# A hybrid decoder block: the mixer's order table made anew

## The reference, cut to what matters

```python
# (A) GLA, per chunk: decay from a low-rank gate, causal scores, a state that is carried on
bc = jnp.cumsum(ac, axis=3)
o_inter = jnp.einsum('bhcd,bhde->bhce', qi * jnp.exp(bi), state)
scores = jnp.einsum('bhid,bhjd,bhijd->bhij', qi, ki, decay)      # decay = exp(bi - bj), causal
o_intra = jnp.einsum('bhij,bhje->bhie', scores, vi)
new_state = jnp.exp(b_last)[..., None] * state + jnp.einsum('bhcd,bhce->bhde', k_dec, vi)
o_gla = rmsnorm(o_gla, gla_norm_g[l]) * jax.nn.silu(g)
# (B) convolution: gate, 31 taps per channel, norm over channel groups, swish
u = c_in * jax.nn.sigmoid(c_gate)
u = causal_depthwise_conv(u, conv_w[l], conv_b[l])
o_conv = jax.nn.silu(channel_group_norm(u, conv_norm_g[l], conv_norm_b[l]))
h = h + jnp.einsum('bse,ed->bsd', jnp.concatenate([o_gla, o_conv], axis=-1), w_out[l])
ff = jnp.square(jax.nn.relu(jnp.einsum('bsd,df->bsf', rmsnorm(h, norm2_g[l]), w_mlp_in[l])))
h = h + jnp.einsum('bsf,fd->bsd', ff, w_mlp_out[l])
```

## Time and profile before

| | |
|---|---|
| median of 3 runs | 2025.66 us (2024.34 to 2025.87) |
| profiled execution, its own time | 2024.25 us |
| its span | 2022.2 us |
| PE busy in the span | 2000.1 us, 99% |
| DVE, ACT, POOL busy | 1473.9, 956.6, 445.9 us |

### The profile page before, as it was taken

The page is one execution under the profiler, slowest core; times in us unless marked ns, Lnnn a source line. Parts: engine busy times, 40 slices in busy tenths (PEclk is TensorE's granted clock), DMA queues, the critical chain, the costliest instruction groups (busy, mean ns, idle before and its releaser), DMA issues.

```text
span 2022.2 us, 27147 instructions
## 1 busy us (share of the span) xinstructions
PE 2000.1 (99%) x9898; PEld 1635.4 (81%) x9898; DVE 1473.9 (73%) x2178; ACT 956.6 (47%) x1361; POOL 445.9 (22%) x593
## 2 busy tenths in 40 slices
PE   8999999999999999999999999999999999999998
PEld 7787778787877778888888888888888888888887
DVE  3899978887878978877789777777664646545475
ACT  4456664355244563565557645554332333323253
POOL 5553475235126441000000000000020201202031
PEclk9999999999999999999999999999999999999999
DMA  6884458555555555444445433335967557565674
GB/s 227 285 289 152 139 202 295 167 168 186 198 200 191 179 208 191 162 146 144 148 163 206 153 122 127 126 121 197 376 231 266 188 203 265 181 220 185 206 239 177
DMA packets 175268, 395.76 MB, mean 196 GB/s; under 512 B 15424, under 2 KB 64672, under 8 KB 174624
## 3 DMA queue, kind: packets, MB, share of 16 engines
q1 hardware_dynamic: 154688, 317.47, 46.3%
q10 hardware_dynamic: 20448, 76.56, 10.8%
HBM read 301.70 MB, written 92.27 MB: 195 GB/s over the span
## 4 chain that ended last, share of the span: by engine, by line
PE 90%; DVE 6%; issue 2%; ACT 2%; POOL 0%; DMA 0%; DVEq 0%; ACTq 0%; POOLq 0%
PE acc L83 24%; PE acc L85 24%; PE acc L84 24%; PE acc L2565 3%; PE acc L2566 3%; PE acc L2567 3%; DVE acc L1724 2%; PE acc L2625 1%; PE acc L2520 1%; PE acc L2519 1%; PE acc L2521 1%; PE acc L2284 1%; ACT ring_hi L1355 1%; PE acc L2658 1%; DVE ring_sum L1869 1%
## 5 line engine op out<-in xcount | busy, mean ns | idle before, releaser
L1986 DVE TENSOR_TENSOR down_lo<-down_raw,down_hi 128x1536 fp32r<-128x1536 f32 x112 | 200.5, 1790 | 231.1 <-ACT down_hi L1441 231.1
L84 PE MATMUL acc<-down_lo,down_hi 128*128 128x512 f32 x896 | 348.5, 389 | 0.0
L83 PE MATMUL acc<-down_hi 128*128 128x512 f32 x896 | 348.5, 389 | 0.0
L85 PE MATMUL acc<-down_hi,down_lo 128*128 128x512 f32 x896 | 348.5, 389 | 0.0
L1441 ACT ACTIVATE down_hi<-down_raw 128x1536 fp32r<-128x1536 f32 x112 | 166.7, 1488 | 360.8 <-PE acc L85 192.9
L1724 DVE SCALAR_TENSOR_TENSOR acc<-u_sb,cw_col,acc 128x512 f32<-128x512 f32 x464 | 312.9, 747 | 0.3
L1355 ACT ACTIVATE ring_hi<-ring_sum 128x512 fp32r<-128x512 f32 x155 | 97.8, 631 | 250.3 <-DVE ring_sum L1869 247.9
L83 PE MATMUL acc<-xT_hi,wt 128*128 128x512 f32 x512 | 203.6, 398 | 0.7 <-ACT q_sb L1534 0.7
L1100 POOL TENSOR_TENSOR rows_a<-rows_a,second 128x512 f32<-128x512 f32 x20 | 25.3, 1296 | 803.6 <-ACT second L1449 655.5
L84 PE MATMUL acc<-xT_lo,wt 128*128 128x512 f32 x512 | 199.5, 390 | 0.0
L85 PE MATMUL acc<-xT_hi,wt 128*128 128x512 f32 x512 | 199.5, 390 | 0.0
(11 more groups left out here) (304 smaller groups left out, 4113.2 us busy)
## 6 DMA issues: line engine op xcount, KB each, us to landing
wt<-w_kept SPq DMA_DIRECT2D x168, 512.0 KB, 3.3
down_raw<-f_kept ACTq DMA_DIRECT2D x109, 512.0 KB, 4.3
raw_w<-in_w_mlp_in SPq DMA_DIRECT2D x32, 1024.0 KB, 5.9
f_kept<-f_tile SPq DMA_DIRECT2D x128, 256.0 KB, 2.0
down_raw<-in_w_mlp_out SPq DMA_DIRECT2D x64, 512.0 KB, 3.6
w_kept<-wt SPq DMA_DIRECT2D x48, 512.0 KB, 5.3
down_raw<-in_w_mlp_out SPq DMA_DIRECT2D x64, 256.0 KB, 3.2
down_more<-f_kept ACTq DMA_DIRECT2D x29, 512.0 KB, 5.3
```

What stands on the lines that cost most here:

```text
L83: nc.tensor.matmul(out, w_hi, x_hi, start=first, stop=False, skip_group_check=onto)
L84: nc.tensor.matmul(out, w_hi, x_lo, start=False, stop=False, skip_group_check=onto)
L85: return nc.tensor.matmul(out, w_lo, x_hi, start=False, stop=last, skip_group_check=onto)
L1986: nc.vector.tensor_tensor(down_lo[slot][:, :], down_raw[d % DOWN_RAW][:, 512:], down_hi[slot][:, :].bitcast(F32), ALU.subtract).then_inc(d ...
```

## The change

Only the list `ORDER` differs. It has 808 entries, where there were 761: the same steps, but the 496 taps, in the same sequence, are cut into 141 entries, where there were 94. The weight units keep their sequence. Against the other entries of the same engine, 59 of PE's 327 steps, 60 of DVE's 212 (taps apart), 95 of ACT's 261 and 31 of POOL's 122 have another place. The diff, cut to the places that the text speaks of:

```diff
-    (-1, "conv_gate_a", 2), (0, "taps", 0, 1, 6), (-1, "make_wz"), (0, "x_load", 2), (-1, "conv_gate", 2),
...
-    (0, "taps", 0, 32, 5), (0, "gate", 0), (0, "qk", 0), (-1, "make_masks", 2), (0, "x_load", 3),
...
-    (0, "gla_scores", 0, 0), (0, "gla_select", 0, 0), (0, "x_tr", 1), (0, "gla_select", 0, 1), (0, "x_tr", 2),
-    (0, "x_tr", 3), (0, "gla_scores", 0, 1), (0, "gla_select", 0, 2), (0, "gla_decayed", 1, 1), (0, "conv_gate_a", 0),
...
-    (0, "gla_out", 1), (0, "gla_decayed", 2, 1), (0, "taps", 1, 46, 13), (0, "gla_select", 2, 0),
-    (0, "gla_decayed", 2, 2), (0, "cn_rstd", 0), (0, "taps", 1, 59, 3), (0, "gla_select", 2, 1), (0, "conv_gate", 2),
...
-    (1, "taps", 0, 12, 6), (0, "gla_out", 2), (0, "gla_heads", 3), (1, "gate", 0), (1, "qk_a", 1),
-    (0, "gla_select", 3, 0), (0, "gla_select", 3, 1), (0, "gla_scores", 3, 0), (0, "cn_var", 1),
...
-    (1, "gla_heads", 3), (1, "gla_decayed", 3, 1), (1, "out", 1, 7), (1, "taps", 1, 30, 4), (1, "out_done", 1, 39),
-    (1, "taps", 1, 34, 6), (1, "gla_out", 2), (1, "store", 1), (1, "conv_gate_a", 0), (1, "conv_gate", 0),
...
-    (2, "gla_decayed", 2, 1), (2, "x_norm", 3), (2, "out_done", 0, 31), (2, "gla_select", 1, 3), (2, "x_tr", 2),
-    (2, "x_tr", 3), (2, "taps", 1, 26, 2), (2, "gla_out", 1), (2, "gla_heads", 2), (2, "gla_factors", 3),
...
-    (2, "gn_mixed", 2), (3, "gla_expo", 1), (3, "v", 3), (3, "gla_factors", 1), (3, "v", 4), (3, "v", 5),
...
-    (3, "up0_part", 2, 3), (3, "cn_mean", 1), (4, "x_norm", 1), (3, "up0_part", 3, 4), (4, "x_tr", 0),
...
-    (3, "mul_sum", 3), (4, "out", 1, 6), (4, "out", 1, 7), (4, "store", 1), (3, "mul_hi", 1), (4, "out_done", 1, 15),
+    (-1, "make_masks", 0), (-1, "make_wz"), (0, "x_load", 0), (-1, "conv_gate_a", 0), (-1, "conv_gate", 0),
...
+    (0, "z"), (0, "qk_a", 0), (0, "taps", 0, 36, 4), (0, "gate", 0), (0, "taps", 0, 40, 5), (0, "qk", 0),
...
+    (0, "taps", 1, 12, 4), (0, "gla_expo", 1), (0, "g_a", 3), (1, "x_load", 0), (0, "g", 3), (0, "x_tr", 0),
+    (0, "x_tr", 1), (0, "gla_select", 0, 0), (0, "gla_select", 0, 1), (0, "gla_scores", 0, 0), (0, "x_tr", 2),
+    (0, "x_tr", 3), (0, "gla_scores", 0, 1), (0, "taps", 1, 16, 2), (0, "conv_gate_a", 0), (0, "gla_select", 0, 2),
...
+    (0, "cn_var", 0), (0, "gla_select", 2, 0), (0, "conv_in_a", 2), (0, "gla_select", 2, 1), (0, "gla_scores", 2, 0),
+    (0, "taps", 1, 52, 10), (0, "conv_in", 2), (0, "conv_gate_a", 3), (1, "taps", 0, 0, 1), (0, "gla_expo", 3),
...
+    (0, "gla_out", 2), (1, "taps", 0, 8, 3), (0, "cn_split", 1), (0, "gla_heads", 3), (1, "taps", 0, 11, 3),
+    (1, "x_sq", 1), (1, "qk_a", 0), (0, "gla_select", 3, 0), (1, "qk", 0), (0, "gla_select", 3, 1), (1, "gate", 0),
+    (1, "taps", 0, 14, 2), (0, "gla_scores", 3, 0), (0, "cn_mean", 1), (1, "taps", 0, 16, 4), (0, "gla_select", 3, 2),
...
+    (1, "gla_decayed", 2, 2), (1, "out_done", 1, 39), (1, "out", 1, 0), (1, "taps", 1, 37, 1), (1, "out", 1, 1),
+    (1, "out", 1, 2), (1, "out", 1, 3), (1, "out", 1, 4), (1, "out", 1, 5), (1, "taps", 1, 38, 1), (2, "x_load", 0),
+    (1, "gla_select", 2, 1), (1, "gla_decayed", 3, 0), (1, "taps", 1, 39, 4), (1, "gla_decayed", 3, 1),
+    (1, "gla_scores", 2, 0), (1, "taps", 1, 43, 3), (1, "gla_factors", 3), (1, "taps", 1, 46, 1), (1, "out", 1, 6),
+    (1, "out", 1, 7), (1, "taps", 1, 47, 2), (1, "store", 1), (1, "taps", 1, 49, 9), (1, "conv_gate_a", 0),
+    (1, "gla_scores", 2, 1), (1, "conv_gate", 0), (1, "conv_in_a", 0), (2, "x_sq", 0), (1, "taps", 1, 58, 1),
...
+    (2, "gla_expo", 2), (1, "cn_silu", 1), (1, "cn_mixed", 1), (2, "x_sq", 2), (2, "res_load", 0),
+    (2, "taps", 1, 26, 2), (2, "gla_select", 1, 2), (2, "gla_select", 1, 3), (2, "gla_scores", 1, 0),
...
+    (3, "qk", 3), (3, "gla_factors", 0), (3, "gla_factors", 1), (3, "gla_decayed", 0, 0), (3, "v", 0), (3, "v", 1),
...
+    (3, "x_tr", 0), (3, "x_tr", 1), (2, "cn_mixed", 1), (3, "cn_rstd", 0), (3, "gla_scores", 1, 0),
...
+    (3, "out", 1, 6), (3, "cn_split", 1), (3, "out", 1, 7), (3, "gla_out", 3), (4, "x_tr", 0), (3, "up0_part", 0, 2),
+    (3, "up0_part", 2, 3), (3, "up0_part", 3, 4), (3, "gn_square"), (3, "gn_sum", 0), (3, "cn_mean", 1),
...
+    (3, "ring", 3), (3, "ring_low", 3), (3, "back", "h12"), (3, "mul_sum", 7), (3, "mul_sum", 1), (3, "mul_sum", 6),
+    (3, "mul_hi", 7), (4, "m_load", 2), (4, "store", 1), (3, "mul_sum", 3), (4, "out_done", 1, 15), (3, "mul_hi", 1),
+    (3, "mul_low", 7),
```

More of the change, by code:

```diff
@@ L130 @@
[L130 to L134, removed]
@@ L140 @@
[L140 to L144, removed]
@@ L145 @@
[L145 to L149, removed]
@@ L185 @@
-    (2, "gla_select", 2, 1), (2, "gla_decayed", 3, 0), (2, "out", 1, 7), (2, "taps", 1, 33, 1),
-    (2, "gla_select", 2, 2), (2, "conv_gate_a", 0), (2, "taps", 1, 34, 7), (2, "out_done", 1, 39),
-    (2, "conv_gate", 0), (2, "gla_select", 2, 3), (2, "taps", 1, 41, 6), (2, "gla_out", 2), (2, "conv_in_a", 0),
-    (2, "gla_decayed", 3, 1), (2, "taps", 1, 47, 10), (2, "gla_select", 3, 0), (2, "conv_in", 0),
-    (2, "gla_decayed", 3, 2), (2, "taps", 1, 57, 4), (2, "gla_select", 3, 1), (2, "conv_gate_a", 1),
@@ L225 @@
-    (3, "taps", 1, 55, 2), (3, "gla_select", 3, 2), (3, "m_split", 1), (3, "taps", 1, 57, 3), (3, "gla_select", 3, 3),
-    (3, "cn_mixed", 0), (3, "out", 1, 7), (3, "taps", 1, 60, 1), (3, "out_done", 1, 39), (3, "gla_out", 3),
-    (3, "taps", 1, 61, 1), (3, "gn_square"), (3, "cn_split", 1), (3, "up0_part", 0, 2), (3, "gn_sum", 0),
-    (3, "up0_part", 2, 3), (3, "cn_mean", 1), (4, "x_norm", 1), (3, "up0_part", 3, 4), (4, "x_tr", 0),
-    (3, "gn_sum", 1), (3, "gn_mixed", 0), (3, "up0_part", 4, 8), (3, "gn_rstd"), (3, "gn_mixed", 1), (3, "cn_var", 1),
@@ new lines @@
+    (0, "gla_select", 3, 3), (1, "taps", 0, 20, 3), (1, "qk_a", 1), (1, "qk", 1), (0, "gla_scores", 3, 1),
+    (1, "gate", 1), (1, "qk_a", 2), (1, "decay"), (0, "gla_out", 3), (0, "gn_square"), (1, "taps", 0, 23, 2),
+    (1, "qk", 2), (1, "taps", 0, 25, 5), (1, "qk_a", 3), (0, "gn_sum", 0), (0, "cn_var", 1), (1, "qk", 3),
+    (0, "gn_sum", 1), (1, "taps", 0, 30, 3), (0, "cn_rstd", 0), (0, "cn_rstd", 1), (1, "v", 0), (1, "v", 1),
+    (1, "v", 2), (1, "v", 3), (1, "taps", 0, 33, 5), (1, "v", 4), (1, "v", 5), (1, "v", 6), (0, "gn_rstd"),
@@ new lines @@
+    (1, "g", 3), (1, "x_tr", 0), (1, "x_tr", 1), (1, "gla_out", 0), (0, "cn_mixed", 1), (1, "out", 0, 0),
+    (1, "gla_heads", 1), (1, "out", 0, 1), (1, "gla_expo", 2), (1, "res_load", 0), (1, "out", 0, 2),
+    (1, "cn_rstd", 0), (1, "taps", 1, 14, 8), (1, "x_sq", 2), (1, "gla_scores", 1, 0), (1, "out", 0, 3),
+    (1, "out", 0, 4), (1, "gla_select", 1, 0), (1, "gla_scores", 1, 1), (1, "gla_select", 1, 1),
+    (1, "gla_factors", 2), (1, "taps", 1, 22, 2), (1, "x_norm", 2), (1, "store", 0), (1, "gla_select", 1, 2),
@@ new lines @@
+    (1, "gla_select", 1, 3), (1, "x_sq", 3), (1, "out", 0, 5), (1, "out", 0, 6), (1, "out", 0, 7),
+    (1, "taps", 1, 24, 3), (1, "x_norm", 3), (1, "taps", 1, 27, 1), (1, "res_load", 1), (1, "out_done", 0, 31),
+    (1, "x_tr", 2), (1, "x_tr", 3), (1, "gla_expo", 3), (1, "taps", 1, 28, 1), (1, "gla_out", 1), (1, "gla_heads", 2),
+    (1, "taps", 1, 29, 8), (1, "gla_decayed", 2, 1), (1, "gla_decayed", 2, 0), (1, "gla_select", 2, 0),
+    (1, "gla_decayed", 2, 2), (1, "out_done", 1, 39), (1, "out", 1, 0), (1, "taps", 1, 37, 1), (1, "out", 1, 1),
@@ new lines @@
+    (1, "conv_in", 2), (1, "conv_gate_a", 3), (2, "taps", 0, 10, 10), (1, "cn_mean", 1), (2, "taps", 0, 20, 3),
+    (1, "conv_gate", 3), (1, "conv_in_a", 3), (1, "gla_select", 3, 0), (1, "gla_select", 3, 1), (2, "taps", 0, 23, 4),
+    (1, "gla_scores", 3, 0), (1, "gla_select", 3, 2), (1, "gla_select", 3, 3), (1, "conv_in", 3),
+    (1, "gla_scores", 3, 1), (2, "z"), (1, "gla_out", 3), (2, "taps", 0, 27, 3), (2, "qk_a", 0), (1, "gn_square"),
+    (2, "qk", 0), (2, "taps", 0, 30, 12), (1, "gn_sum", 0), (1, "cn_var", 1), (1, "cn_rstd", 1), (2, "gate", 0),
@@ new lines @@
+    (2, "qk_a", 1), (2, "qk", 1), (2, "taps", 0, 42, 1), (1, "gn_sum", 1), (2, "gate", 1), (2, "decay"),
+    (2, "taps", 0, 43, 1), (1, "gn_rstd"), (2, "gla_expo", 0), (2, "qk_a", 2), (2, "qk", 2), (2, "qk_a", 3),
+    (2, "taps", 0, 44, 3), (2, "qk", 3), (2, "taps", 0, 47, 1), (2, "v", 0), (2, "taps", 0, 48, 11),
+    (2, "gla_factors", 0), (2, "taps", 0, 59, 3), (2, "v", 1), (2, "gla_expo", 1), (2, "v", 2), (2, "v", 3),
+    (2, "gla_decayed", 0, 0), (2, "gla_decayed", 0, 1), (2, "v_done", 15), (2, "gla_decayed", 0, 2), (2, "v", 4),
@@ new lines @@
+    (2, "taps", 1, 12, 3), (2, "gla_scores", 0, 1), (2, "gla_select", 0, 2), (2, "gla_select", 0, 3),
+    (2, "cn_var", 0), (2, "x_norm", 1), (2, "cn_rstd", 0), (2, "taps", 1, 15, 1), (2, "g_a", 2), (2, "x_load", 2),
+    (2, "g", 2), (2, "g_a", 3), (2, "x_load", 3), (2, "g", 3), (2, "x_tr", 0), (2, "x_tr", 1), (2, "gla_out", 0),
+    (2, "taps", 1, 16, 6), (2, "gla_heads", 1), (2, "taps", 1, 22, 1), (2, "gla_select", 1, 0), (2, "taps", 1, 23, 3),
```

(26 more changed lines are left out.)

185 lines of the change are left out of this document (78 added, 107 removed).

## The result

The changed list takes 2039.14 us in the median (2036.0 to 2042.2, 4 runs) against 2025.51 before: ratio 1.0071, interval 1.0058 to 1.0084. It is slower by 14 us, where 7 less were forecast. The profiled execution took 2038.66 us, its span 2036.6.

What follows compares the result with a forecast made beforehand. PE was taken as the bound, busy 2000.1 of 2022.2 us, so only its idle time could be won. Gains 11.0 - 1.7 - 0.6 - 1.5 = 7.2 us less, median 2018.5 us, range 2014.2 to 2025.0.

Steps and rivals of the forecast that it cites:

- part 3: New DVE neighbours beside POOL: two-SBUF-input instructions collide at 1.1 us each; 1.5 us taken, bounds -1 and 13.
- the small rival, the first: Six or so thin-slack points hit by DVE-POOL collisions, 5 us come back, 2023.5 us; chance 0.15.
- Part 1: PE's mixer waits, each by its place in the new list: gains of 11.0 us, 1.7 coming back.
- the eleven waits: PE's gaps in the mixer, 36 to 807 us, set by the list's order: 11.0 us removable.
- Part 2: Steps pulled forward that may block a queue: make_wz costs nothing, out_done is covered, the mixer's end costs 0.6 us.
- The second: Pulled-forward out_done idles DVE about 10 us in blocks 1 and 2, its work piles up: 2036 us; chance 0.07.
- The third: All of PE's mixer waits go and nothing comes back: 2014.7 us; chance 0.15.
- the fourth: The list moves the waits elsewhere in equal amount, DVE bounding block 0: 2024 to 2026 us; chance 0.07.

Runs made afterwards that it cites:

- narrowed pair: GpSimd's instructions of the two norms cut to 64 of 512 columns, on the changed list and on the kernel before: 2018.35 us and 2023.03 us.
- narrowed run: The changed list with GpSimd's instructions of the two norms cut to 64 of 512 columns: 2018.35 us, ratio 0.9969.
- second of the last three kernels: Changed list with six GpSimd waits and some steps moved back, plus x_sq and x_norm 1 and 2 early again in block 0: 2024.62 us, ratio 1.0001.

## Why the prediction was wrong

The step that failed is part 3, the DVE beside POOL: taken at 1.5 us, with an upper bound of 13. The narrowed pair puts it near 19 us: the edit gives the new list 20.8 and the old one 1.4, and 1.8 of the difference is the wait at out(4,0,2). That is over the upper bound too. It was mis-sized in two ways, and the clock, whose loss is in these 19 us, was left out.

- Its size. I priced single hits of 1.1 us and took one or two, "since only a small part of the DVE's work is of this kind". DVE's busy time grew by 24 us. The hits come in rows: eight sums in 5.79 us for 2.63, fifteen exponents in 8.1 for 3.2, four norms of gn_rstd in 5.1 for about 3 alone (3.8 in the kernel before). The earlier trace rows already had the long ones (1376 ns), and I did not ask for each step of the new list what POOL does in those us.
- Its place. I charged a hit only "where a chain has no slack", and counted points with under 0.5 us. But delays on one in-order queue add up: between 223 and 273 us the sums, the norms and the exponents of two chunks take about 12 us more than alone, 10 more than before, and that ate far more slack. cn_mean(1,0), which waits for the last tap of a pair, was on none of my lists.
- The clock was put at nothing, as it is 1.00 in the earlier trace rows. Behind waits of 2.5 and 5.7 us it fell, and by the estimate above that is 3.4 of the 3.7 us of longer busy time.

The page "SBUF — State Buffer" of the Trainium skill, section "Who interferes with whom", which stood there as speaking against the change, is borne out: the loser waits for the whole of the other's instruction (1.37 us beside 1.34). I had named it and then gave it the small rival.

Part 1 was right in its mechanism, but for the wait for k_endT, which was a collision of the old list: of the eleven waits only the one at gn_sum(3,0) is left whole at its place, and without most of the collisions PE's idle time is 4.2 us, where 3.5 were forecast; gn_sum(3,0) stayed because a normalisation and two products ahead of the state's update on the DVE take 1.6 us longer beside POOL (1.80 for 1.28 and 2.39 for 1.28); the update itself takes 1.48 as before. Its worth is 4.7 us as the narrowed pair measures it, against the 8.7 that my sum has without part 3 (11.0 - 1.7 - 0.6; the gains as listed add up to 10.75). The first v unit of block 1 starts at 237.4 and not at 230, and at 232.2 in the narrowed run. Part 2: the loads of make_wz landed later than I took, ACT stood 7.2 us for them until 44.1, and PE still has no wait for a weight unit near 47 us. The MLP kept its length.

Of the rivals the first had the mechanism but 5 us for it and a time of 2023.5; it should have been the forecast, with three and a half times the price or more. The second, which was to cover the slower side, did not happen: DVE stands 2.95 us before out_done(1,1) and 1.1 before out_done(2,1), not 10, and PE has no wait at gla_out(1,2). The third and the fourth did not happen.

Left open: the clock. It fell to 0.66 after 2.46 us of idling at gn_sum(0,0), and in the run with cn_mean later it stayed at 1.00 after 2.47 us at the same place. What differs was not tried. Open too is whether any order keeps the 4.7 us with the whole work; none of the runs here did.

## What to carry to other kernels

When a list of steps for in-order engines is made anew, price for each instruction of the DVE with two inputs in SBUF what POOL runs in the same us, and add the delays up along the queue; slack must be held against the sum, not against a hit. Work that did not collide here (taps that add to PSUM, 731 to 757 ns in the changed kernel) is what to put beside POOL's. To test such a cause cheaply, let the other engine wait: no order changes, and the wait on PE goes or stays. Judge it by that wait and by the lengthened rows, not by the whole time alone, since what hangs on the engine that waits comes later.

## What was not expected

A TensorE wait of 5.7 us cost about 1.8 us more in clock, by the estimate above: 0.50 and 0.82 in the ten us around it. And POOL loses as well: the products of chunk (0,0) took 5.5 us beside the DVE's normalisation, where they took 3.0 before, and a weight unit behind them came 1.4 us late. In the second of the last three kernels, with the normalisation moved away, they take 3.6 us and that wait is gone.
